# Recurrence channels in a new order, and the gate products across chunks as twelve 32x32 fp32 matmuls

## What is computed

```python
def rglru_layer(x, norm_g, w_in, conv_w, conv_b, wr, br, wi, bi, lam, w_out):
    u = rmsnorm(x, norm_g) @ w_in                     # 1024 -> 2 * 1536
    xb, gate = u[..., :LRU_WIDTH], u[..., LRU_WIDTH:]
    xb = causal_depthwise_conv(xb, conv_w, conv_b)    # 4 taps per channel
    xs = xb.reshape(bsz, seq, LRU_BLOCKS, LRU_BLOCK_W)     # 16 blocks of 96
    r = sigmoid(einsum('bshi,hij->bshj', xs, wr) + br)     # block-diagonal
    i = sigmoid(einsum('bshi,hij->bshj', xs, wi) + bi)
    log_a = -LRU_C * r * softplus(-lam)
    a = exp(log_a)
    b = sqrt(-expm1(2.0 * log_a)) * (i * xb)          # sqrt(1 - a*a) * i * x
    hs = scan(h = a * h + b over the sequence)
    return x + (hs * silu(gate)) @ w_out              # 1536 -> 1024
```

## Time and profile before

| | us |
|---|---|
| time before, median of 3 runs | 1107.65 (1107.54 to 1107.73) |
| the profiled execution's own time | 1107.12 |
| its span, first to last instruction | 1105.3 |
| PE busy in it | 1096.1 (99%) |
| DVE busy | 755.9 (68%) |
| ACT busy | 559.4 (51%) |
| granted TensorE clock, mean | 0.999 of full |

### The profile page before, as it was taken

The page is one execution under the profiler, slowest core; times in us unless marked ns, Lnnn a source line. Parts: engine busy times, 40 slices in busy tenths (PEclk is TensorE's granted clock), DMA queues, the critical chain, the costliest instruction groups (busy, mean ns, idle before and its releaser), DMA issues.

```text
span 1105.3 us, 14356 instructions
## 1 busy us (share of the span) xinstructions
PE 1096.1 (99%) x5216; PEld 869.2 (79%) x5216; DVE 755.9 (68%) x1276; ACT 559.4 (51%) x953; POOL 121.5 (11%) x170
## 2 busy tenths in 40 slices
PE   9999999999999999999999999999999999999997
PEld 6787787887677778867777878888888888888886
DVE  7887977777677765465545545537697697796795
ACT  6667667465676644254434433325453453453455
POOL 2000000030323312032112210003000000000003
PEclk9999999999999999999999999999999999999999
DMA  6322322332111123311222222323501701602401
GB/s 229 118 76 95 113 78 96 99 109 88 58 58 58 58 82 110 105 58 58 96 76 97 76 76 95 96 96 112 211 20 43 281 1 58 247 1 76 172 1 76
DMA packets 30054, 103.79 MB, mean 94 GB/s; under 512 B 3488, under 2 KB 3872, under 8 KB 29984
## 3 DMA queue, kind: packets, MB, share of 16 engines
q1 hardware_dynamic: 29552, 102.26, 27.2%
q10 hardware_dynamic: 432, 0.62, 0.2%
HBM read 100.24 MB, written 2.10 MB: 93 GB/s over the span
## 4 chain that ended last, share of the span: by engine, by line
PE 97%; DVE 1%; issue 0%; ACT 0%; POOL 0%; DVEq 0%; POOLq 0%
PE ps L903 24%; PE ps L904 24%; PE ps L905 24%; PE ps L863 4%; PE ps L864 4%; PE ps L865 4%; PE ps L1007 3%; PE ps L1022 3%; PE ps L1053 2%; PE ps L1047 1%; PE ps L810 1%; PE ps L944 0%; PE ps L812 0%; PE ps L814 0%; PE ps L936 0%
## 5 line engine op out<-in xcount | busy, mean ns | idle before, releaser
L903 PE MATMUL ps<-xgh,wh 128*128 128x512 f32 x847 | 336.7, 398 | 0.8 <-issue 0.8
L905 PE MATMUL ps<-xgh,wl 128*128 128x512 f32 x847 | 330.2, 390 | 0.0
L904 PE MATMUL ps<-xgl,wh 128*128 128x512 f32 x847 | 329.9, 390 | 0.0
L1416 DVE TENSOR_TENSOR wl<-raw,wh 128x1024 fp32r<-128x1024 f32 x148 | 188.7, 1277 | 41.1 <-ACT wh L1092 38.8
L1092 ACT ACTIVATE wh<-raw 128x1024 fp32r<-128x1024 f32 x148 | 155.0, 1050 | 78.7 <-PE ps L905 58.1
L903 PEld LDWEIGHTS ps<-xgh,wh 128*128 128x128 f32 x847 | 159.1, 188 | 38.0 <-issue 5.4
L905 PEld LDWEIGHTS ps<-xgh,wl 128*128 128x128 f32 x847 | 159.0, 188 | 33.8
L904 PEld LDWEIGHTS ps<-xgl,wh 128*128 128x128 f32 x847 | 159.2, 188 | 32.3 <-issue 1.0
L1961 POOL TENSOR_SCALAR Pt<-Pt,stat 128x256 f32<-128x256 f32 (+2 forms) x128 | 74.0, 590 | 275.8 <-DVE stat L1717 200.3
L1300 ACT ACTIVATE Pt<-Pt,stat 128x256 f32<-128x256 f32 (+2 forms) x128 | 64.3, 503 | 60.5 <-DVE stat L1685 23.1
L863 PE MATMUL ps<-wh,fh 128*128 128x512 f32 x224 | 87.1, 389 | 0.0
(11 more groups left out here) (244 smaller groups left out, 1685.8 us busy)
## 6 DMA issues: line engine op xcount, KB each, us to landing
raw<-wst SPq DMA_DIRECT2D x148, 512.0 KB, 3.4
b<-wdn SPq DMA_DIRECT2D x32, 512.0 KB, 6.8
bst<-nbias SPq DMA_DIRECT2D x8, 256.0 KB, 3.4
xt<-xT SPq DMA_DIRECT2D x3, 512.0 KB, 8.0
outT<-xtok SPq DMA_DIRECT2D x3, 512.0 KB, 2.6
sq<-fin SPq DMA_DIRECT2D x2, 256.0 KB, 3.9
cstt<-cst SPq DMA_DIRECT2D x1, 448.0 KB, 5.5
raw<-wst SPq DMA_DIRECT2D x1, 320.0 KB, 5.3
```

The lines of the kernel that those rows point to most:

```text
L903: e.matmul(o, high, a, start=(k == 0), stop=False)
L904: e.matmul(o, high, b, start=False, stop=False)
L905: e.matmul(o, low, a, start=False, stop=stop).then_inc(tile_done, 1)
L1416: e.tensor_tensor(wl_t[:, v % NHL, :], src, f32(wh_t[:, v % NHL, :]), ALU.subtract).then_inc(lo_done, 1)
```

## The change

Five things are changed, all in the first layer.

1. **Channel order** (`channel_order`, `CHANNELS`): in each group, chunk m now holds block m (96 channels) and, in its rows 32m to 32m+31 (`PIECE[m]`), a third of block 3. The host permutes weights, biases and taps accordingly. Products from chunk to chunk are now only between these 32-row pieces.
2. **The gates' block**: six own tiles in the order gr, gi of each chunk, then `gates_cross`: 12 matmuls, each 32 rows by 32 columns by 512 tokens, in plain fp32 on `xs` and a new constant tile `crossw`. They stand in two turns of six. Within a turn all six have a different pair of row and column strips and a different bank; a wait on `cross_half` stands between the turns, since two of them add to the same strip of the same bank. The six gates' last step now all end with the second turn (`end`). The four over tiles are gone from the weight stream: 16 tiles, that is two units of 149 in the ring.
3. **The root**: `cc` = tanh of a quarter of the exponent (`PL2`), the root is taken of it at once, and DVE multiplies by (1 + a) after the root (L1453 of after) where it multiplied by (1 + a*a) before. The Square and `qq` are gone; `tii` has three buffers.
4. **Order and ticks**: `wa` 0's three tiles for g = 2 and 3 now stand behind the group's first `conv` instead of ahead of it; `UNIT_AT` is a table for units 5 to 31; `gate_tick`, `root_tick`, `y_low`, the taps' ticks and a few more are new.
5. **One more DMA**: `crossw` (256 KB) on SP's queue at tick 26.

```diff
-        c = 3 * g
-        for own, over in (([("gr", c), ("gi", c)], 2), ([("gr", c + 1), ("gr", c + 2)], 0), ([], 3), ([("gi", c + 1), ("gi", c + 2)], 1)):
...
+        names = [(kind, c) for c in range(3 * g, 3 * g + 3) for kind in ("gr", "gi")]
+        for name in names:
+            self.take(name)
+            self.tiles.append((name, 0, True))
+        self.at_cross[len(self.tiles) - 1] = g
+        for name in names:
+            self.end[name] = len(self.tiles) - 1
...
+            def gates_cross(g):
+                q.wait_ge(cross_in, 16)
+                for c in range(3 * g, 3 * g + 3):
+                    q.wait_ge(conv_done[c % 2], 3 * (c // 2) + 3)
+                for turn in range(2):
+                    if turn:
+                        q.wait_ge(cross_half, g + 1)
+                    for m in range(3):
+                        for n, kind in enumerate(("gr", "gi")):
+                            skip = (turn + n) % 2
+                            to = (m + 1 + skip) % 3
+                            done = e.matmul(bank[ch.bank[kind, 3 * g + to]][PIECE[to]], crossw[PIECE[m], g, 2 * n + skip, :],
+                                            xs[(3 * g + m) % 6][PIECE[m]], start=False, stop=False, skip_group_check=True)
+                    done.then_inc((cross_half, tile_done)[turn], 1)
...
-            ch.take_in(("wa", 0), 7)
-        if g > 1:
-            ch.run(("wa", 0), 3 * g - 6, 3 * g - 3, 12)
...
             for c in range(3 * g, 3 * g + 3):
                 ch.one(("conv", c), KD)
+                if g == 2 and c == 6:
+                    ch.take_in(("wa", 0), 7)
+                if g > 1 and c == 3 * g:
+                    ch.run(("wa", 0), 3 * g - 6, 3 * g - 3, 12)
...
+        for u in range(5, 32):
+            UNIT_AT[u] = ch.units[u][1] - (15.0, 18.0, 17.0, 17.0, ...)[u - 5]
...
-            return end["gi", c] + 1.2 + 3.5 * (c % 3 > 1)
+            return end["gi", c] + (2.2, 4.2, 7.2)[c % 3]
...
-                e.activation(cc[c % 3], trr, ACT.Tanh, scale=drvc(PL4 + c, PL4 + c + 1), bias=drvc(PL4 + c, PL4 + c + 1)).then_inc(t_done, 1)
-                yield gate_tick(c) + 3.0
-                q.wait_ge(a_done, c + 1)
-                q.wait_ge(c2_done, c - 1)
-                e.activation(qq[c % 2], aa[c % 3], ACT.Square).then_inc(q2_done, 1)
+                e.activation(cc[c % 3], trr, ACT.Tanh, scale=drvc(PL2 + c, PL2 + c + 1), bias=drvc(PL2 + c, PL2 + c + 1)).then_inc(t_done, 1)
...
-                e.scalar_tensor_tensor(cc[c % 3], qq[c % 2], 1.0, cc[c % 3], ALU.add, ALU.mult).then_inc(c2_done, 1)
...
+                    q.wait_ge(a_done, c + 1)
+                    q.wait_ge(c_done, c + 1)
+                    e.scalar_tensor_tensor(cc[c % 3], aa[c % 3], 1.0, cc[c % 3], ALU.add, ALU.mult).then_inc(c2_done, 1)
```

More of the change, by code:

```diff
@@ L23, with channel_order @@
 EXP_AND_TANH = "exp_and_others"
-ORDER = (1, 0, 2)
-CHUNKS = [3 * g + m for g in range(4) for m in ORDER]
+BW = 96
+PIECE = [slice(32 * m, 32 * m + 32) for m in range(3)]
+def channel_order():
+    order = []
+    for g in range(4):
+        blocks = np.arange(4 * BW * g, 4 * BW * (g + 1)).reshape(4, BW)
+        for m in range(3):
+            order += [blocks[m, :PIECE[m].start], blocks[3, PIECE[m]], blocks[m, PIECE[m].start:]]
+    return np.concatenate(order)
+CHANNELS = channel_order()
 PAR = {}
@@ L150, in gates @@
     def gates(self, g):
-        c = 3 * g
-        for own, over in (([("gr", c), ("gi", c)], 2), ([("gr", c + 1), ("gr", c + 2)], 0), ([], 3), ([("gi", c + 1), ("gi", c + 2)], 1)):
[L155 to L166, removed]
+        names = [(kind, c) for c in range(3 * g, 3 * g + 3) for kind in ("gr", "gi")]
[5 more added lines that the diff above has]
+            self.end[name] = len(self.tiles) - 1
+            self.n_act += 1
+            self.frees[name] = ("act", self.n_act)
     def group(self, names, k, ks):
@@ L624, in build @@
         LOW_AFTER[2] = 0.5
[L625 to L635, removed]
+        for u in range(5, 32):
+            UNIT_AT[u] = ch.units[u][1] - (15.0, 18.0, 17.0, 17.0, 17.0, 18.0, 18.0, 15.0, 15.0, 17.0, 15.0, 15.0, 18.0, 17.0, 13.0, 15.0, 13.0, 15.0, 15.0, 13.0, 15.0, 15.0, 17.0, 15.0, 15.0, 15.0, 15.0)[u - 5]
+            LOW_AFTER[u] = 1.75
         for u in range(len(UNIT_AT) + 1, n_units):
             if u < form_no[0, "P1", 0]:
-                UNIT_AT[u] = max(8.0 * u - 20.0, UNIT_AT[u - 1] + 5.0)
+                UNIT_AT[u] = max(ch.units[u][1] - 20.0, UNIT_AT[u - 1] + 5.0)
             else:
@@ L2005, in tiles, with gate_blocks @@
     return w.reshape(k // 128, 128, m // 128, 128).transpose(2, 0, 1, 3)
+def gate_blocks(a):
+    full = np.zeros((2, LW, LW), np.float32)
+    for n, name in enumerate(("a_gate_r_w", "a_gate_i_w")):
+        for b in range(16):
+            j = slice(BW * b, BW * b + BW)
+            full[n, j, j] = a[name][0, b]
+    return full[:, CHANNELS][:, :, CHANNELS].reshape(2, 12, 128, 12, 128)
 def weight_stream(a):
@@ L2080, in weight_stream, with cross_weights @@
     return np.ascontiguousarray(s.reshape(-1, UT, 128, 128).transpose(0, 2, 1, 3).reshape(-1, 128, UT * 128))
+def cross_weights(a):
+    full = gate_blocks(a)
+    cross = np.zeros((128, 4, 4, 32), np.float32)
+    for g in range(4):
+        for m in range(3):
+            for n in range(2):
+                for skip in range(2):
+                    to = (m + 1 + skip) % 3
+                    cross[PIECE[m], g, 2 * n + skip] = full[n, 3 * g + m, PIECE[m], 3 * g + to, PIECE[to]]
+    return cross
 def down_weights(w):
```

112 lines of the change are left out of this document (50 added, 62 removed).

## The result

| | median us | runs |
|---|---|---|
| before | 1107.69 | 4, 1107.54 to 1109.29 |
| after | 1100.24 | 4, 1100.16 to 1100.59 |

The ratio is 0.9931 (95% interval 0.9915 to 0.9947): 7.45 us less. The profiled execution of after has a time of its own of 1100.17 us and a span of 1098.4 us, at a granted clock of 0.998.

A forecast was written before the change was run, and what follows sets the result against it. PE, busy 99% of the span, was taken to bound the kernel. Gates' blocks -6.9, new wait +0.96 and early wait -0.14 gave -6.1 us: 1107.65 to 1101.6 us, range 1100.3 to 1108.6.

The forecast's parts named there:

- six strips at once: Cross turns: six distinct pairs of strips work together, a turn being two waves of 0.43 us; 1101.6 us, chance 0.74.
- the second rival: Cross turns: a row strip serves one matmul at a time, four waves a turn, nothing saved; 1108.4 us, chance 0.11.
- the program-order rival: Cross turns: matmuls start in program order, seven waves a turn, 17.2 us more in all; 1118.8 us, chance 0.07.
- The fourth rival: A cover fails: late weight copy on ACT, or DVE late, 1 us in several groups; 1103 to 1107 us, chance 0.08.
- The block: Gates of each group: 6.48 us, saving 1.70 in three groups and 1.79 in group 0, 6.9 us together.
- Its second wave starts 0.11 + 0.43 later: First cross turn: the second wave starts 0.11 us (shape change) plus 0.43 us (one instruction) behind the first.
- the 6.4 that the prediction named as its sign: Sign of being right: a gates' block of 6.4 to 6.6 us from first `xsh` matmul to next product.
- The hand-over within PE: Wait on `cross_half` between the turns: 0.11 us, taken from PE to ACT, with bounds 0 and 0.2.
- The new wait: Behind group 2's gates, group 3's first `conv` waits until ACT has read ps3: 0.96 us, once.
- The early wait: PE's step at unit 4, near 30 us, waiting for a DVE subtraction, goes away: worth 0.14 us.
- The rest at nothing: ACT, DVE (85% busy between group 1's and group 2's gates, from 83%), other banks and `crossw` DMA cost nothing, being covered.
- the first case's terms: Six-at-once range: `cross_half` and starts at lower bounds give 7.4 saved and 1100.9 us; at upper bounds, 1104.4 us.

The follow-up runs named there:

- three_tiles: Changed kernel with each turn's six cross products laid on three pairs of row and column strips instead of six, sums in wrong channels: 1106.98 us.
- wa0_first: Changed kernel with, in group 3 alone, the three output tiles of unit `wa` 0 ahead of the convolution again: 1099.57 us, ratio 0.9933.
- early_old: Changed kernel with the early order put back (unit 5 at tick 23, group 0's taps at their former ticks): 1100.72 us, ratio 0.994.
- square_back: Changed kernel with the root's change alone undone (ScalarE squares again, VectorE multiplies ahead of the root): 1100.59 us, ratio 0.9939.
- root_alone: Kernel before with the root's change alone (no square, VectorE multiplies behind the root): 1107.51 us, ratio to before 1.0001.
- before_again: The kernel before, unaltered, profiled a second time: 1107.83 us in its profiled execution.
- no_cross: Changed kernel without its cross products, gates computed from the own parts alone: 1096.10 us, a single execution.
- after_again: The changed kernel, unaltered, run on another occasion: 1100.55 us, ratio 0.9939.
- best: wa0_first with the sum of the second head also placed one tick later in VectorE's order: 1099.43 us, ratio 0.9929.
- between: wa0_first with the second and third matmul of the last own tile moved between the two cross turns: 1099.79 us, ratio 0.9929.
- no_cross_wa0: wa0_first without the cross products, gates computed from the own parts alone: 1095.52 us, a single execution.

## Why the prediction was near and yet outside its range

- **What bounds, and six strips at once.** Right. A turn is two waves, and the second rival fell with three_tiles, the program-order rival with the first halves of six matmuls ahead of the first one's second half. The Trainium skill, TensorE: Matmul & The Clock Gate, "The mechanism", says that matmuls start strictly in order. The trace of after does not agree where the two halves of an fp32 matmul are concerned, as the earlier trace rows did not; of matmuls taken whole it shows nothing against it. The fourth rival did not happen either.
- **The block.** The step "Its second wave starts 0.11 + 0.43 later" failed in size: it took 0.453 us. The 0.11 was read in the earlier trace rows behind the first pair of an over tile, a tile of 32*128, and carried over to a 32x32 tile; there it is under 0.03, twice a block, against which the spread of a wave's members (0.034 us, costed at nothing) takes a little back. That made 6.36 instead of 6.48 us, also under the 6.4 that the prediction named as its sign. The earlier trace rows had hinted at it: two waves with both extras should have taken 0.63 us there, and took 0.59. The saving is 1.91 in group 0 and 8.18 - 6.36 = 1.82 in the others, 7.4 us for 6.9. The hand-over within PE, borrowed from PE to ACT, held: 0.696 - 0.587 = 0.11 us.
- **The new wait.** Right in place and nearly in price: 1.41 - 0.52 = 0.89 for 0.96 us, and wa0_first takes it away.
- **The early wait.** Right in cause, too small in price: 0.27 for 0.14 us (early_old).
- **The rest at nothing.** Right for the root and its covers: square_back differs by 0.03 us from after in the fixed part of the trace, root_alone by 0.05 from before_again and 0.16 from before. But VectorE's cover was thinner than costed. The walk had 85% between the gates of group 1 and group 2; the changed kernel shows 38.79 us of 43.22, 90%, and 82% in the next stretch:

```profile
79.89:123.11 43.22, 43.11 (x206) 34.04 (x204) 38.79 (x51) 28.45 (x39) 0.00 (x0) 1.00 0.30 98
```

No wait came of it here; no_cross shows how near one was.

- **The sum.** With the measured sizes it is -7.4 + 0.9 - 0.3 = -6.8 us, against the -6.1 of the forecast; the block's size is 0.5 of that difference. The later runs give 1107.36 - 1100.55 = 6.8. From the median of 1107.65 on which the prediction stood this gives 1100.9, inside the range. For the profiled execution at 1100.17 us what is left lies ahead of the block: it reaches the 41st matmul at 14.93 us, after_again at 15.24, and all behind is equal within 0.1 us. That the median of 1100.24 lies low for the same reason is likely and not shown. The range had no room for it: its low end came from the first case's terms and hardly more. These terms also give 1101.1 and not 1100.9 (7.3 saved), and the second rival's sum has 0.2 where the early wait was priced 0.14; neither changes the forecast.

So the mechanism was right and the failed step is the size of the extra behind a change of shape (0.54 us forecast to the second wave, 0.453 measured), and beside it a range whose low end had no room for how medians of the same kernel move between occasions (0.3 us). With a range that left room for that, the same sum would have held. Why the early weight copy lands at different times was not tried.

## What to carry to other kernels

An extra that a trace shows at one shape of the array is not a constant: read it at the shape that comes, or carry both ends into the sum. Where the bound engine gets shorter in a place, ask how much room the lists of the other engines have there: here 2.28 us taken from PE in one block would have brought 0.65. A wait is priced as its step and the slower step behind it. Ready work of the same shape removed one (wa0_first); moving the late piece took the wait along (best); and cover that changed the array's shape cost as much as the wait (between).

## What the runs showed of the hardware

- Six fp32 matmuls of 32 rows on 32 columns, each on its own pair of a row and a column strip, start 7 ns apart and together take the time of one. Two on one pair follow one another, half behind half, at 0.43 us (three_tiles).
- TensorE's clock was at 1.2 GHz for some 3 us in two places, each behind a long step from one start to the next: 2.80 us in no_cross (at once, from 126.7 us), 2.32 us in wa0_first (from 11.3 us). Behind steps of 1.2 us in before and after, of 1.8 us in no_cross_wa0 and of 2.15 us in before_again the next full steps were 0.23 us, the clock at 2.4 GHz. These are single cases; no run here tests what decides between them.
